# Sliding-window attention of a two-layer encoder: unnormalised probabilities turned, values by token rows, band and maximum fused

## The reference

```python
def swa_sink_attention(q, k, v, sinks):
    bn, s_len, hq, dh = q.shape
    hk = k.shape[2]
    grp = hq // hk
    n = s_len // CHUNK
    qc = q.reshape(bn, n, CHUNK, hk, grp, dh)

    def band(t):
        t = t.reshape(bn, n, CHUNK, hk, dh)
        parts = [jnp.pad(t, ((0, 0), (j, 0), (0, 0), (0, 0), (0, 0)))[:, :n]
                 for j in range(WINDOW_CHUNKS - 1, -1, -1)]
        return jnp.concatenate(parts, axis=2)

    kb, vb = band(k), band(v)
    src_chunk = jnp.arange(n)[:, None] - jnp.repeat(jnp.arange(WINDOW_CHUNKS - 1, -1, -1), CHUNK)[None, :]
    valid = src_chunk >= 0
    s = jnp.einsum('bnqkgd,bnskd->bnkgqs', qc, kb).astype(F32) * (dh ** -0.5)
    s = jnp.where(valid[None, :, None, None, None, :], s, -jnp.inf)
    sink = jnp.broadcast_to(sinks.astype(F32).reshape(hk, grp)[None, None, :, :, None, None], s.shape[:-1] + (1,))
    p = jax.nn.softmax(jnp.concatenate([s, sink], axis=-1), axis=-1)[..., :-1]
    o = jnp.einsum('bnkgqs,bnskd->bnqkgd', p.astype(vb.dtype), vb)
    return o.reshape(bn, s_len, hq * dh)
```

## Time and profile before

| what | before |
|---|---|
| median of 3 runs | 2755.05 us |
| lowest and highest of them | 2750.62 and 2755.51 us |
| the profiled execution's own time | 2751.75 us |
| its span, first to last instruction | 2749.9 us |
| PE busy, share of the span | 2608.1 us, 95% |
| DVE busy | 1656.4 us, 60% |
| ACT busy | 969.6 us, 35% |
| mean granted TensorE clock | 0.970 of full speed |
| the stage of the change, first band addition to the last result copied | 1899.85 to 1961.98 us |

### The profile page before, as it was taken

One profiled execution on the slowest core, in us unless ns is written; L12 is line 12 of the kernel. 1 busy time (PEld: TensorE's weight loads), 2 busy tenths in 40 slices (PEclk: granted clock), 3 DMA queues, 4 the chain that ended last, 5 costly groups with the idle time before them and its releaser, 6 DMA issues.

```text
span 2749.9 us, 32120 instructions
## 1 busy us (share of the span) xinstructions
PE 2608.1 (95%) x12096; PEld 2073.1 (75%) x12096; DVE 1656.4 (60%) x2647; ACT 969.6 (35%) x1615; POOL 263.6 (10%) x268
## 2 busy tenths in 40 slices
PE   8999969888998899999999999898899999999998
PEld 7676748788655587888888878676687888888787
DVE  4379996766465367666564364663758566553444
ACT  3322311111344344333333243454634333332333
POOL 3015624443000000000001000000000000000000
PEclk9999988987799999999999999999999999999999
DMA  5121100000100233232326433111141332336443
GB/s 162 46 69 39 39 15 1 0 0 1 46 1 23 65 96 115 77 92 77 92 80 219 146 131 126 39 41 37 39 138 62 92 92 62 92 96 226 138 138 108
DMA packets 207167, 217.27 MB, mean 79 GB/s; under 512 B 12497, under 2 KB 174305, under 8 KB 203569
## 3 DMA queue, kind: packets, MB, share of 16 engines
q1 hardware_dynamic: 204080, 196.13, 22.8%
q0 software_dynamic: 2944, 19.24, 1.9%
HBM read 172.35 MB, written 42.47 MB: 78 GB/s over the span
## 4 chain that ended last, share of the span: by engine, by line
PE 81%; DVE 13%; issue 4%; ACT 2%; POOL 0%; DMA 0%; DVEq 0%; SPq 0%; POOLq 0%; ACTq 0%
PE ps L329 21%; PE ps L330 21%; PE ps L331 21%; DVE met L1978 4%; PE ps L2708 2%; DVE bT L1955 2%; PE ps L2190 2%; PE ps L2203 1%; PE ps L2685 1%; PE ps L423 1%; PE ps L2199 1%; PE ps L2696 1%; PE ps L1056 1%; PE ps L417 1%; PE ps L1765 1%
## 5 line engine op out<-in xcount | busy, mean ns | idle before, releaser
L318 DVE TENSOR_TENSOR wlo<-wraw,whi 128x1024 fp32r<-128x1024 f32 x152 | 185.8, 1224 | 371.1 <-ACT whi L312 370.7
L312 ACT ACTIVATE whi<-wraw 128x1024 fp32r<-128x1024 f32 x166 | 174.8, 1054 | 353.0 <-PE ps L331 335.6
L329 PE MATMUL ps<-ahi,whi 128*128 128x512 f32 x704 | 276.0, 392 | 6.3 <-DVE hT L956 4.1
L330 PE MATMUL ps<-alo,whi 128*128 128x512 f32 x704 | 274.7, 390 | 0.0
L331 PE MATMUL ps<-ahi,wlo 128*128 128x512 f32 x704 | 274.6, 390 | 0.0
L329 PE MATMUL ps<-uhi,whi 128*128 128x512 f32 x608 | 245.5, 404 | 14.7 <-DVE bT L1965 6.3
L329 PE MATMUL ps<-q_T,whi 128*128 128x512 f32 x640 | 249.2, 389 | 1.6 <-ACT upr L757 1.6
L331 PE MATMUL ps<-q_T,wlo 128*128 128x512 f32 x640 | 249.1, 389 | 0.0
L330 PE MATMUL ps<-q_T,whi 128*128 128x512 f32 x640 | 249.1, 389 | 0.0
L329 PE MATMUL ps<-q_B,whi 128*128 128x512 f32 x608 | 239.0, 393 | 2.4 <-DVE q_B L488 2.4
L330 PE MATMUL ps<-ulo,whi 128*128 128x512 f32 x608 | 238.8, 393 | 0.0
(11 more groups left out here) (465 smaller groups left out, 4861.7 us busy)
## 6 DMA issues: line engine op xcount, KB each, us to landing
wraw<-in_ffn_w_down_dram SPq DMA_DIRECT2D x88, 512.0 KB, 3.5
wraw<-in_ffn_w_gate_dram SPq DMA_DIRECT2D x44, 512.0 KB, 5.3
araw<-acts SPq DMA_DIRECT2D x88, 256.0 KB, 3.7
wraw<-in_ab_w_in_dram SPq DMA_DIRECT2D x24, 512.0 KB, 3.8
park<-hT POOLq DMA_DIRECT2D x3, 4096.0 KB, 11.4
wraw<-in_ffn_w_up_dram SPq DMA_DIRECT2D x24, 512.0 KB, 5.2
acts<-sgA SPq DMA_DIRECT2D x12, 1024.0 KB, 4.6
raw<-in_ffn_w_up_dram SPq DMA_DIRECT2D x20, 512.0 KB, 3.9
```

Of the source, the lines that this page charges most:

```text
L312: nc.scalar.activation(as_raw(whi[:, t.slot, :]), raw, ACT.Copy).then_inc(S("w_high"), 1)
L318: eng.tensor_tensor(as_raw(wlo[:, t.slot, :]), raw, as_raw(whi[:, t.slot, :]).bitcast(F32), ALU.subtract).then_inc(S("w_split"), 1)
L329: nc.tensor.matmul(dst, wh, xh, start=start, stop=False, **kw)
L330: nc.tensor.matmul(dst, wh, xl, start=False, stop=False, **kw)
```

## The change

The band's addition, the scale of -1/8 and the reduction become one operation per head (4 in place of 2 additions and one reduction; the sign is turned, so it takes a minimum). `d_p` is turned without having been divided by the sum. `values` exchanges its operands: `d_pt` of one head (128 columns) is stationary and `vrow` (64 columns) is moving, so the result has token rows on the partitions; 8 matmuls per unit in place of 4. `rows` on DVE multiplies it by the reciprocal of the sum into the new buffer `d_o`. `turn_back` on PE transposes `d_o` in two 128x128 pieces into the other half of the same PSUM bank, and `result` copies them to `dq`, now on DVE. PE's order is scores(n+2), turn(n), values(n-1), turn_back(n-2); ACT's is soft(n+1), move(n); DVE's is result(n-3), bias(n+1), rows(n-2), denominator(n).

```diff
--- before.py
+++ after.py
@@ -157,6 +157,7 @@
             "t_lo": ("bv_ready", 1), "a_landed0": ("go_spread", 4), "a_landed1": ("kv_sq", 1),
             "a_landed2": ("h_back", 16), "a_landed3": ("h_back_rest", 16), "a_hi": ("ql_done", 8),
             "a_lo": ("at_ol", 2 * NB), "d_part": ("at_rs", NB), "d_added": ("at_y_turned", NB), "h_again": ("go_sq", 4),
+            "d_back": ("kv_diag", 1),
         }
         sems = {}
 
@@ -1193,6 +1194,7 @@
         d_s = at("d_s", [P, 2, 4, 192], 148 * KB)
         d_pt = at("d_pt", [P, 2, 2, 4, P], 172 * KB)
         d_p = at("d_p", [P, 2, 4, 256], 180 * KB)
+        d_o = at("d_o", [P, 2, 256], 204 * KB)
         wax = at("wax", [P, 8, P], 56 * KB)
         spot = [0]
 
@@ -1446,7 +1448,7 @@
 
             def turn(n):
                 b, g = divmod(n, 2)
-                pe.wait_ge(*after("d_p", n + 1))
+                pe.wait_ge(*after("d_exp", 5 * n + 4))
                 if n >= 1:
                     pe.wait_ge(*after("d_pt", n))
                 for kt in range(1 if b == 0 else 0, 2):
@@ -1460,25 +1462,33 @@
                 pe.wait_ge(*after("d_pt", n + 1))
                 if n >= 2:
                     pe.wait_ge(*after("d_y", n - 1))
-                kts = [1] if b == 0 else [0, 1]
-                for odd in range(2):
-                    for kt in kts:
-                        last = pe.matmul(bank(6 + n % 2)[64 * odd:64 * odd + 64, 0:256],
-                                         vrow[:, b - 1 + kt, g * 64:g * 64 + 64],
-                                         d_pt[:, n % 2, kt, odd:4:2, :], start=kt == kts[0], stop=kt == 1)
+                for h in range(4):
+                    for kt in range(1 if b == 0 else 0, 2):
+                        last = pe.matmul(bank(6 + n % 2)[:, h * 64:(h + 1) * 64], d_pt[:, n % 2, kt, h, :],
+                                         vrow[:, b - 1 + kt, g * 64:g * 64 + 64], start=kt == (b == 0), stop=kt == 1)
                 last.then_inc(S("d_out"), 1)
+
+            def turn_back(n):
+                pe.wait_ge(*after("d_p", n + 1))
+                for a in range(2):
+                    last = pe.transpose(bank(6 + n % 2)[:, 256 + a * P:256 + (a + 1) * P],
+                                        d_o[:, n % 2, a * P:(a + 1) * P], ident[:, :])
+                last.then_inc(S("d_back"), 1)
 
             pe.wait_ge(S("dkx_landed"), 32)
             pe.wait_ge(*after("dv_moved", 1))
+            pe.wait_ge(S("d_zero"), 1)
             scores(0)
             scores(1)
-            for n in range(2 * NB):
+            for n in range(2 * NB + 2):
                 if n + 2 < 2 * NB:
                     scores(n + 2)
-                turn(n)
-                if n:
+                if n < 2 * NB:
+                    turn(n)
+                if 1 <= n <= 2 * NB:
                     values(n - 1)
-            values(2 * NB - 1)
+                if n >= 2:
+                    turn_back(n - 2)
 
         def swa_act(act):
             def soft(n):
@@ -1486,9 +1496,10 @@
                 act.wait_ge(*after("d_nm", n + 1))
                 if n >= 2:
                     act.wait_ge(*after("d_turned", n - 1))
+                    act.wait_ge(*after("d_den", 2 * n - 2))
                 k0 = d_keys(b)
                 for h in range(4):
-                    act.activation(d_p[:, n % 2, h, 64 + k0:256], d_s[:, n % 2, h, k0:192], ACT.Exp, scale=0.125,
+                    act.activation(d_p[:, n % 2, h, 64 + k0:256], d_s[:, n % 2, h, k0:192], ACT.Exp, scale=-1.0,
                                    bias=d_nm[n % 2][:, h:h + 1], accum_out=d_sum[n % 2][:, h:h + 1]).then_inc(S("d_exp"), 1)
                 act.activation(d_es[n % 2][:, :], d_es[n % 2][:, :], ACT.Exp).then_inc(S("d_exp"), 1)
 
@@ -1501,20 +1512,11 @@
                 act.activation(d_pt[:, n % 2, k0:2, :, :].rearrange("p k a n -> p k (a n)"), PS[:, 4 + k0:6, :],
                                ACT.Copy).then_inc(S("d_pt"), 1)
 
-            def result(n):
-                b, g = divmod(n, 2)
-                act.wait_ge(*after("d_out", n + 1))
-                act.activation(dq[:, 2 * g:2 * g + 2, b * P:(b + 1) * P],
-                               bank(6 + n % 2)[:, 0:256].rearrange("p (a n) -> p a n", a=2), ACT.Copy).then_inc(S("d_y"), 1)
-
             soft(0)
             for n in range(2 * NB):
                 if n + 1 < 2 * NB:
                     soft(n + 1)
                 move(n)
-                if n:
-                    result(n - 1)
-            result(2 * NB - 1)
 
         def swa_dve(dve):
             def bias(n):
@@ -1523,38 +1525,52 @@
                 dve.wait_ge(*after("d_scores", n + 1))
                 if n >= 2:
                     dve.wait_ge(*after("d_exp", 5 * n - 5))
-                for a in range(2):
-                    ins = dve.tensor_tensor(
-                        d_s[:, n % 2, a:4:2, k0:192],
-                        bank(2 * (n % 2) + a)[:, 0:384].rearrange("p (h k) -> p h k", h=2)[:, :, k0:192],
-                        band[:, k0:192].unsqueeze(1).broadcast_to([P, 2, 192 - k0]), ALU.add)
+                for h in range(4):
+                    at_ = (h // 2) * 192
+                    ins = dve.tensor_tensor_reduce(
+                        d_s[:, n % 2, h, k0:192], bank(2 * (n % 2) + h % 2)[:, at_ + k0:at_ + 192], band[:, k0:192],
+                        -0.125, 3.0e38, ALU.add, ALU.min, d_m[n % 2][:, h:h + 1])
                 ins.then_inc(S("d_biased"), 1)
                 dve.wait_ge(*after("d_biased", n + 1))
-                dve.tensor_reduce(d_m[n % 2][:, :], d_s[:, n % 2, :, k0:192], AX.X, ALU.max).then_inc(S("d_max"), 1)
-                dve.wait_ge(*after("d_max", 2 * n + 1))
-                dve.scalar_tensor_tensor(out=d_m[n % 2][:, :], in0=d_m[n % 2][:, :], scalar=0.125,
-                                         in1=sink[:, 4 * g:4 * g + 4], op0=ALU.mult, op1=ALU.max).then_inc(S("d_max"), 1)
-                dve.wait_ge(*after("d_max", 2 * n + 2))
-                dve.tensor_tensor(d_es[n % 2][:, :], sink[:, 4 * g:4 * g + 4], d_m[n % 2][:, :], ALU.subtract)
-                dve.tensor_scalar(d_nm[n % 2][:, :], d_m[n % 2][:, :], -1.0, None, ALU.mult).then_inc(S("d_nm"), 1)
-
-            def norm(n):
-                b, g = divmod(n, 2)
-                k0 = d_keys(b)
+                dve.scalar_tensor_tensor(out=d_nm[n % 2][:, :], in0=sink[:, 4 * g:4 * g + 4], scalar=-1.0,
+                                         in1=d_m[n % 2][:, :], op0=ALU.mult, op1=ALU.min).then_inc(S("d_max"), 1)
+                dve.wait_ge(*after("d_max", n + 1))
+                dve.tensor_tensor(d_es[n % 2][:, :], sink[:, 4 * g:4 * g + 4], d_nm[n % 2][:, :],
+                                  ALU.add).then_inc(S("d_nm"), 1)
+
+            def denominator(n):
                 dve.wait_ge(*after("d_exp", 5 * n + 5))
                 dve.tensor_tensor(d_sum[n % 2][:, :], d_sum[n % 2][:, :], d_es[n % 2][:, :], ALU.add).then_inc(S("d_den"), 1)
                 dve.wait_ge(*after("d_den", 2 * n + 1))
+                if n >= 2:
+                    dve.wait_ge(*after("d_p", n - 1))
                 dve.reciprocal(d_inv[n % 2][:, :], d_sum[n % 2][:, :]).then_inc(S("d_den"), 1)
+
+            def rows(n):
+                dve.wait_ge(*after("d_out", n + 1))
                 dve.wait_ge(*after("d_den", 2 * n + 2))
-                dve.tensor_tensor(d_p[:, n % 2, :, 64 + k0:256], d_p[:, n % 2, :, 64 + k0:256],
-                                  d_inv[n % 2][:, :].unsqueeze(2).broadcast_to([P, 4, 192 - k0]), ALU.mult).then_inc(S("d_p"), 1)
-
-            dve.wait_ge(S("d_zero"), 1)
+                if n >= 2:
+                    dve.wait_ge(*after("d_back", n - 1))
+                dve.tensor_tensor(d_o[:, n % 2, :].rearrange("p (h d) -> p h d", d=64),
+                                  bank(6 + n % 2)[:, 0:256].rearrange("p (h d) -> p h d", d=64),
+                                  d_inv[n % 2][:, :].unsqueeze(2).broadcast_to([P, 4, 64]), ALU.mult).then_inc(S("d_p"), 1)
+
+            def result(n):
+                b, g = divmod(n, 2)
+                dve.wait_ge(*after("d_back", n + 1))
+                dve.tensor_copy(dq[:, 2 * g:2 * g + 2, b * P:(b + 1) * P],
+                                bank(6 + n % 2)[:, 256:512].rearrange("p (a n) -> p a n", a=2)).then_inc(S("d_y"), 1)
+
             bias(0)
-            for n in range(2 * NB):
+            for n in range(2 * NB + 3):
+                if n >= 3:
+                    result(n - 3)
                 if n + 1 < 2 * NB:
                     bias(n + 1)
-                norm(n)
+                if 2 <= n < 2 * NB + 2:
+                    rows(n - 2)
+                if n < 2 * NB:
+                    denominator(n)
```

## The result

The changed kernel takes 2764.57 us (median of 20 runs) against 2755.66 for the kernel before (20 runs beside them); the ratio is 1.0034, with a 95% interval of 1.0025 to 1.0042. It is slower by some 9 us. The profiled execution has a span of 2758.9 us against 2749.9.

What follows compares the result with a forecast made beforehand. DVE bounded the stage at 3.66 us per unit; afterwards a two-unit loop would, at 4.13. Start +1.7, units 4 to 15 +5.1, end +2.4: +9.2 on 2751.75 gives 2761.0, as a median 2763 us; 8-in-10 range 2755 to 2775.

Steps and rivals of the forecast that it cites:

- start, to the band operations of unit 4: First part of the stage, PE working at 1.2 GHz until about 1911.8 us: 1.7 us longer.
- units 4 to 15: Middle of the stage: eleven units at 4.13 us in place of 3.66, 5.1 us longer.
- end: From the last unit's band operations to the output projection's first split: 12.3 us in place of 9.9, +2.4.
- PE takes over from DVE: In the stage, PE's work per unit becomes 3.89 us, above the 3.66 that DVE set; DVE falls to 2.5.
- The loop through result ahead of bias: Waits from result through bias, soft, move, turn, values, turn_back to result: 8.26 us for two units, 4.13 per unit.
- The fused operation at 0.28: On DVE, each of four fused operations per unit takes 0.28 us at 192 columns; bounds 0.20 and 0.42.
- The clock: PE's granted clock in the stage: low at its start, rising at about 1911.8 us, 1.00 from about 1912.
- The rival in which it stays low for most of the stage: PE's clock stays at 1.2 GHz: 7.5 us per unit, about 2809 us in all; chance 0.07.
- DVE below 75% busy, waiting for turn_back ahead of its copies, neighbouring units 3.9 and 4.4 us apart by turns: Signs expected in the stage's profile after the change, with units 4.1 us apart on average.
- hidden loads: Rival: PE's weight loads hide behind other work, values cost 0.89 to 1.02 us; total 2753 to 2756; chance 0.13.
- Faster, with ACT's 2.99 ruling: Rival: the loop does not close and ACT sets 2.99 us per unit; about 2747 us; chance 0.06.
- POOL's clearing at 0: POOL's clearing of `d_p`, awaited ahead of scores(0), costs 0; without cover by DVE's weight splitting, 0.5 us.

Runs made afterwards that it cites:

- e3: Changed kernel with the operands of values as before (output not the reference's): stage 63.0 us, ratio 0.9995 to the kernel before.
- e2: Changed kernel with DVE's order turned, bias(n+1) ahead of result(n-3): stage 65.6 us, ratio 1.0009 to the kernel before.
- e4: Changed kernel with the band's addition and the maximum as separate operations again: stage 75.9 us, ratio 1.0061 to the kernel before.
- e5: Changed kernel with three extra matmuls on PE at the stage's end, output unchanged: stage 69.7 us, ratio 1.0017 to the kernel before.
- e1: Kernel before with only the fused band operation per head added: stage 52.8 us, ratio 0.9961 to the kernel before.
- e7: Changed kernel with DVE's order turned and values' operands as before (output not the reference's): stage 55.9 us, ratio 0.9978 to the kernel before.

## Why the prediction was right

It forecast 2763 us and a loss of 9.2 (2763 lies between 2751.75 + 9.2 and the first median, 2755.05, + 9.2); measured are 2764.57 and 8.9. The terms against the two profiles, one execution each:

| term | forecast | measured |
|---|---|---|
| start, to the band operations of unit 4 | +1.7 | +1.4 (13.42 - 12.01) |
| units 4 to 15 | +5.1 | +3.7 (43.99 - 40.32) |
| end | +2.4 | +2.4 (12.29 - 9.90) |
| behind the stage | 0 | +2.6 (97.5 - 94.9) |
| ahead of the stage | 0 | -1.4 (1898.41 - 1899.85) |

- **PE takes over from DVE**: right. The 0.111 us per instruction of the earlier trace rows held nearly (0.108: 1.73 for sixteen, 1.78 taken), and e3 shows what the exchange cost. PE's own unit is 3.83 (e2), 3.89 taken.
- **The loop through result ahead of bias**: right in its members and its order, and shown by e2 (opening it helps), e4 (lengthening it hurts by half) and e3. Its length was 8.26 as summed and 8.03 as measured. From turn_back's start to DVE's copy it is 0.26 where 0.40 was taken, and from the band operations to ACT's first exponential 1.62 where 1.69 was taken; the other steps are within 0.05. Over eleven units this makes 1.4 us.
- **The fused operation at 0.28**: right; DVE's unit too (2.5 us, and 12.48 us busy in the five units of the 20 us window).
- **The clock**: right for the stage. It fell at its start and was back at about 1910.4 us, 12.0 us after the first band operation; I had let it rise at 1911.8, 11.95 us after. The rival in which it stays low for most of the stage did not come.
- **The end**: the length was right. What I did not follow is what it does next. In the last 10 us PE waits again and again for ACT and DVE, and then 2.06 us for the output projection's first operand; the clock falls there, and the 2.6 us come on top. The windows show this and e5 agrees. The prediction had only the stage's own windows in view and took the projection as unchanged. So it lacked a term of 2.6 us, and had the loop 1.4 us and the start 0.3 us too long. The profiled execution also happened to save 1.4 us ahead of the stage, and lost 0.4 behind the norm. The errors cancel, and that the total agrees to some tenths is partly luck.
- **"DVE below 75% busy, waiting for turn_back ahead of its copies, neighbouring units 3.9 and 4.4 us apart by turns"**: 62%, yes, and 3.8 and 4.2 (copies at 1935.58, 1939.42 and 1943.61).
- **The rivals**: hidden loads are excluded by the 0.108 us per load that the trace shows. "Faster, with ACT's 2.99 ruling" did not come, and its reasoning was wrong: with the loop open, PE's own unit, which the prediction itself put at 3.89, still rules and not ACT's. e2 shows it at 3.83, slower than before. A unit bounded by ACT, at 3.03, came only in e1, with the fused operation and without the rest.
- **A slip in the sum**: 11 x (4.13 - 3.66) is 5.2 and not 5.1. It moves the total by 0.1 us.
- **POOL's clearing at 0**: right. PE's first scores wait for it and come 0.6 us later behind the transposes ahead of them than before (1895.89 - 1893.00 against 1896.74 - 1894.44), but the first band operation comes 5.41 us behind those transposes in both.

## What to carry to other kernels

Where one engine's row is without gaps, look at how much its neighbours have free before you move work off it. Here ACT was 88% and PE 83% busy in the middle of the stage. Some 0.9 us less per unit on DVE alone gained 9.4 us; in the full change, with 0.7 us more on PE for values, 0.2 for turn_back and the loop, the stage lost 7.5. A change in several parts should be timed part by part; its best part can be hidden under the others. When a copy is put ahead of the next unit's first operation in an engine's order, follow what it waits for back to that engine: if the path returns there, its length over the units that it spans is a bound that no busy share shows. And a matmul's price must be read by its form: the same products cost 0.7 us more with 128 stationary and 64 moving columns than with 64 and 256. When the stages of two profiles are compared, compare their middles, starts and ends apart, with the granted clock beside each.

## What the runs showed of the hardware

A fall of the clock at the end of one stage costs in the next. The granted clock was 0.55 to 0.60 in the first 8 us of the output projection in the changed kernel, after PE had waited 0.61, 0.85 and 2.06 us in the 6 us ahead, and the distance behind the stage was 97.5 us. With three extra matmuls in those waits (e5) the clock was 1.00 and the distance 94.9.

The waits do not decide it alone. In the 6 us ahead of the projection PE waited 0.18 and 2.03 us in the kernel before, 0.91 and 2.03 in e1, and the clock stayed up (94.9 both). With the three waits of the changed kernel, the clock fell in e2 (96.3 us), e4 (97.7) and e7 (97.6), and it did not in e3 (94.9). So these runs do not say in which execution it falls, and the exact condition stays open.
